# Differential attention in a decoder step: one mask, maximum and scaling for both components, rotation's additions on GpSimd, scores that wait per tile, weights transposed inside the value projection

## The reference, cut to what matters

```python
def diff_mix(q, k_parts, v_parts, masks, lam):          # per block of 128 queries
    scores = []
    for kp, mk in zip(k_parts, masks):
        s = jnp.einsum('bqhcd,bkhcd->bhcqk', q, kp).astype(F32) * ATTN_SCALE   # c: two components of 64
        s = jnp.where(mk, s, -jnp.inf)                  # causal
        scores.append(s)
    p = jax.nn.softmax(jnp.concatenate(scores, axis=-1), axis=-1)
    w = p[:, :, 0] - lam * p[:, :, 1]
    ...                                                 # o = w @ v

def diff_layer(...):
    q = rope(p[..., :QK_B].reshape(bsz, t_, H_B, 2, DK_B), pos)
    z = p[..., QK_B:]
    o = head_rmsnorm(attend(q, lam), subln) * (1.0 - lam_init)
    y = (o.reshape(bsz, t_, D_B).astype(x.dtype) * jax.nn.silu(z)) @ w_out
    return x + y
```

## Time and profile before

| | us |
|---|---|
| time, median of 3 runs | 2083.9 (2082.17 to 2084.59) |
| the profiled execution | 2088.54 |
| its span, first to last instruction | 2086.9 |
| TensorE busy in the span | 1802.2 (86%) |
| VectorE busy | 1164.0 (56%) |
| ScalarE busy | 821.2 (39%) |
| GpSimd busy | 402.1 (19%) |
| attention phase, from its first matmul to the last of its value projections | 955 to 1638 |

### The profile page before, as it was taken

How to read it: one execution, slowest core, us unless ns; L and a number is a source line. 1 busy time by engine, 2 the same in 40 slices (tenths; PEclk the granted TensorE clock), 3 DMA queues, 4 the chain that set the end, 5 groups by cost and what they waited for, 6 DMA issues and landing times. The chain is left out here.

```text
span 2086.9 us, 39907 instructions
## 1 busy us (share of the span) xinstructions
PE 1802.2 (86%) x12755; PEld 1650.1 (79%) x12755; DVE 1164.0 (56%) x3291; ACT 821.2 (39%) x2244; POOL 402.1 (19%) x847
## 2 busy tenths in 40 slices
PE   4399999999999585998999998999999688888598
PEld 4399899899999564997889898898989566665398
DVE  4444544444443354336767677676777466666533
ACT  5233333333333222133535435354354356666401
POOL 1022222222222121011313222122232100101101
PEclk8699999999999766998999999999999788989699
DMA  4213113113211134222111120211200267776522
GB/s 118 64 32 65 29 35 64 34 30 64 36 29 14 38 87 122 86 103 69 41 53 32 31 63 11 53 32 31 62 11 13 70 220 274 248 250 239 158 73 84
DMA packets 157013, 165.21 MB, mean 79 GB/s; under 512 B 12315, under 2 KB 134267, under 8 KB 156915
## 3 DMA queue, kind: packets, MB, share of 16 engines
q1 hardware_dynamic: 152610, 159.85, 25.9%
q0 software_dynamic: 1184, 4.23, 0.8%
q10 hardware_dynamic: 3120, 0.01, 0.1%
HBM read 138.69 MB, written 25.37 MB: 79 GB/s over the span
## 5 line engine op out<-in xcount | busy, mean ns | idle before, releaser
L837 PE MATMUL PS<-WH,XH 128*128 128x384 f32 (+1 forms) x1024 | 329.0, 321 | 2.7 <-DVE WORK L749 2.7
L837 PE MATMUL PS<-WL,XH 128*128 128x384 f32 (+1 forms) x1024 | 317.5, 310 | 0.0
L837 PE MATMUL PS<-WH,XL 128*128 128x384 f32 (+1 forms) x1024 | 317.2, 310 | 0.0
L837 PEld LDWEIGHTS PS<-WH,XH 128*128 128x128 f32 x1024 | 194.1, 190 | 3.6 <-DVE WORK L749 3.2
L1464 PE MATMUL PS<-WH,XH 128*128 128x256 f32 (+1 forms) x576 | 165.7, 288 | 36.0 <-DVE WL L1334 31.3
L837 PEld LDWEIGHTS PS<-WL,XH 128*128 128x128 f32 x1024 | 194.3, 190 | 0.0
L837 PEld LDWEIGHTS PS<-WH,XL 128*128 128x128 f32 x1024 | 193.7, 189 | 0.0
L1464 PE MATMUL PS<-WL,XH 128*128 128x256 f32 (+1 forms) x576 | 164.8, 286 | 0.0
L1464 PE MATMUL PS<-WH,XL 128*128 128x256 f32 (+1 forms) x576 | 163.6, 284 | 0.0
L1890 PE MATMUL PS<-WH,XH 128*128 128x256 f32 x512 | 154.9, 303 | 4.3 <-ACT WORK L1618 2.3
L1890 PE MATMUL PD<-WH,XH 128*128 128x256 f32 x512 | 151.0, 295 | 3.3 <-PEq L142 3.3
(11 more groups left out here) (368 smaller groups left out, 4645.6 us busy)
## 6 DMA issues: line engine op xcount, KB each, us to landing
RAW<-in_cache_k SPq DMA_DIRECT2D x64, 512.0 KB, 4.6
WORK<-in_cache_v SPq DMA_DIRECT2D x64, 512.0 KB, 4.4
RAW<-in_w_in_a SPq DMA_DIRECT2D x40, 512.0 KB, 6.2
RAW<-in_w_in_b SPq DMA_DIRECT2D x16, 512.0 KB, 6.5
RAW<-in_w_kv SPq DMA_DIRECT2D x16, 512.0 KB, 5.3
out<-WORK SPq DMA_DIRECT2D x16, 512.0 KB, 3.2
WORK<-in_x_prompt SPq DMA_DIRECT2D x8, 512.0 KB, 4.6
WORK<-d_G SPq DMA_DIRECT2D x8, 512.0 KB, 13.3
```

Source lines behind the costliest of these rows:

```text
L837: last = nc.tensor.matmul(bank[:, 0:n], x[:, k, tt], reg(w)[:, k, :], start=(i == 0), stop=(i == 3 * KT - 1))
```

## The change

It touches `attention_phase` alone, and one PSUM allocation that joins PD's two halves so that one instruction can address both components.

1. VectorE: mask, maximum and scaling of a tile are one instruction each for both components (`maxima`), so three instead of six. `weights` and `output`, which stood between the components, follow. The two reciprocals become one.
2. ScalarE: the exponential of c = 1 goes first, then the copy of the transposed weights, then c = 0; both wait for the joint scaling.
3. TensorE: `scores(t)` waits once for both exponentials of t-1, and for the rests of the tiles that it reads; the matmuls of the components alternate. The general wait before `scores(0)` goes, a smaller one stands in t = 1.
4. TensorE: `turn_weights(t-1)` moves from before the value projection of t+1 into its middle.
5. Rotation: the negative sine product is formed on VectorE, and two additions per tile move to GpSimd, which writes q and k to their places; the copy on GpSimd goes. VectorE's wait for its own rotation goes, and it waits for GpSimd before the next tile's products. SyncE waits for GpSimd before it sends keys.
6. The sample tile of sweep 1 is projected into bank B_O instead of PD, and some order in `sweep1` of VectorE and GpSimd changes.

```diff
-            QKR = take(2, 2, P)
+            QKR = take(2, P)
-            S = [PD[c][:, :, :].rearrange("p a n -> p (a n)") for c in range(2)]
+            S = PDT[:, :, :, :].rearrange("p c a n -> p c (a n)")
...
+                    def exponentials(h, t, c):
+                        n = (t + 1) * P
+                        act.activation(PR[:, c, 0:n], S[:, c, 0:n], ACT.Exp, scale=ATTN_SCALE, bias=nm[:, c:c + 1],
+                                       accum_out=sm[:, c:c + 1]).then_inc(ex, 1)
                     def sweep2(h, last):
...
-                            if 1 <= t < NT:
-                                weights(h, t - 1)
                             if t < NT:
+                                act.wait_ge(mxs, NT * h + t + 1)
+                                act.wait_ge(ww, NT * h + t)
+                                exponentials(h, t, 1)
+                                if t >= 1:
+                                    weights(h, t - 1)
                                 if t > 4:
                                     act.wait_ge(wt[1], 4 * h + (t - 4))
-                                for c in range(2):
-                                    act.wait_ge(mxs, 2 * (NT * h + t) + c + 1)
-                                    ...
+                                exponentials(h, t, 0)
...
-                        for t in range(NT):
-                            pool.wait_ge(rope, NB * h + t + 1)
-                            g.tensor_copy(KR[:, t, :], QKR[:, t % 2, 1, :]).then_inc(kr, 1)
-                            if t == 0 and before is not None:
+                        for t in range(NB):
+                            pool.wait_ge(rot, NB * h + t + 1)
...
+                            g.tensor_tensor(q_to..., RA[0:n, 0:4, :], RB[0:n, 0:4, :], ALU.add)
+                            g.tensor_tensor(k_to..., RA[0:n, 4:8, :], RB[0:n, 4:8, :], ALU.add).then_inc(rope, 1)
+                            if t == 1 and before is not None:
                                 root(before, NT - 1)
...
-                        links.link(v.tensor_tensor(RB[0:n, 1:8:2, :], src[:, 0:8:2, :], sin, ALU.mult))
-                        ...
-                        v.tensor_tensor(dst[:, 0:8:2, :], RA[0:n, 0:8:2, :], RB[0:n, 0:8:2, :], ALU.subtract)
-                        v.tensor_tensor(dst[:, 1:8:2, :], RA[0:n, 1:8:2, :], RB[0:n, 1:8:2, :], ALU.add)\
-                         .then_inc(rope, 1)
-                        dve.wait_ge(rope, NB * h + t + 1)
+                        dve.wait_ge(rope, NB * h + t)
+                        v.tensor_tensor(RA[0:n, :, :], src, cos, ALU.mult)
+                        v.scalar_tensor_tensor(RB[0:n, 0:8:2, :], src[:, 1:8:2, :], -1.0, sin, ALU.mult, ALU.mult)
+                        v.tensor_tensor(RB[0:n, 1:8:2, :], src[:, 0:8:2, :], sin, ALU.mult).then_inc(rot, 1)
...
+                    def maxima(h, t):
+                        n = (t + 1) * P
+                        dve.wait_ge(sc, NT * h + t + 1)
+                        links.link(v.tensor_tensor(S[:, :, n - P:n], S[:, :, n - P:n],
+                                                   cst[:, C_MB:C_MB + P].unsqueeze(1).to_broadcast([P, 2, P]), ALU.add))
+                        links.link(v.tensor_reduce(mx, S[:, :, 0:n], AX, ALU.max, negate=True))
+                        v.tensor_scalar(nm, mx, ATTN_SCALE, None, ALU.mult).then_inc(mxs, 1)
+                    def combine(h, t):
+                        n, b = (t + 1) * P, t % 2
+                        dve.wait_ge(ex, 2 * (NT * h + t) + 2)
+                        links.link(v.reciprocal(rc[:, b, :], sm))
+                        links.link(v.scalar_tensor_tensor(cf, sm[:, 0:1], nl, rc[:, b, 1:2], ALU.mult, ALU.mult))
+                        v.scalar_tensor_tensor(PR[:, 0, 0:n], PR[:, 1, 0:n], cf, PR[:, 0, 0:n], ALU.mult, ALU.add)...
                     def sweep2(h, last):
                         for t in range(NB):
                             if t < NT:
+                                maxima(h, t)
+                            if 4 < t < NT:
+                                weights(h, t - 1)
+                            if t >= 2:
                                 output(h, t - 2)
...
-                    heads(dve, sweep1, sweep2, tail, links, 10 + 8 * 2 * 2 + 16)
+                    heads(dve, sweep1, sweep2, tail, links, 1 + 8 * 4)
...
                     def scores(h, t):
+                        pe.wait_ge(ex, 2 * NT * h + 2 * t)
+                        for b in range(2):
+                            pe.wait_ge(trf[b], 4 * h + t // 2 + 1)
+                        for at in range(0, width, 512):
...
+                            for q, k in ((QTH, KTH), (QTH, KTL), (QTL, KTH)):
+                                for c in range(2):
...
                         for t in range(1, NT):
                             scores(h, t)
+                            values_free(t + 1)
+                            project(1, t + 1, B_V, (0, KT // 2))
...
                             turn_weights(h, t - 1)
-                            project_values(t + 1)
+                            project(1, t + 1, B_V, (KT // 2, KT))
                             if t >= 2:
                                 turn_output(h, t - 2)
                             weigh(h, t - 1)
```

166 lines of the change are left out of this document (75 added, 91 removed).

## The result

| | before | changed |
|---|---|---|
| median (lowest to highest), 4 runs each | 2083.03 us (2081.76 to 2084.59) | 2062.06 us (2061.76 to 2067.26) |
| ratio, 95% interval | | 0.9905 (0.9887 to 0.9922) |
| second comparison, on the chip of *rotation_dve*, *sep_cut_order* and *turn_first* | 2079.11 us | 2061.81 us, 0.9914 (0.9892 to 0.9936) |
| the profiled execution (its span) | 2088.54 us (2086.9) | 2067.26 us (2065.6) |
| attention phase, first projection to last output transposed | 696.0 us (955.21 to 1651.17) | 675.9 us (951.26 to 1627.12) |

The kernel became faster, inside the stated range (2036 to 2080) and inside the first case's own range, but by 21 us and not by the 32 of the sum. The attention phase alone gave 20.1 of it; the phases ahead of it were 4.0 shorter in that one execution and those behind it 2.8 longer, which the change doesn't touch.

The account below looks back on a forecast made before the run. It took VectorE's program fetch at the loop's return, a VectorE-ScalarE ring in sweep 2 and TensorE in sweep 1 as bounds. Terms summed to -32.4 us: 2088.5 to 2056.1, scaled to the runs' median 2052; range 2036 to 2080.

Parts of the forecast that it names:

- the first case: VectorE's late restart at the loop's return is gone; likeliest 2052 us, own range 2036 to 2068, chance 0.72.
- stall: Sweep 2 of heads 1 to 6: VectorE's program fetch at the loop's return disappears with a shorter loop; -38.4 us.
- ring: Sweep 2, VectorE and ScalarE: both exponentials now wait for the joint maximum; +1.4 us a head, +10 in all.
- last head's ring: Last head, without cuts: the general wait before its first scores goes and the end comes earlier; -1 us.
- end of sweep 2: TensorE's next-head projection follows the last exponential sooner, about 1.0 us in each of 7 heads; -7 us.
- the clock: TensorE's longer wait before `turn_output(5)` at sweep 2's end lowers its clock in one head of three; +4 us.
- 153 is nearer to the lower end: VectorE's loop of 153 counted instructions lies nearer 131 (no gap) than 203 (gap), so the gain is taken whole.
- that rival (2078): VectorE's fetch gap at the loop's return stays despite the shorter loop; 2078 us (2070 to 2086), chance 0.19.
- The rotation: Sweep 1: TensorE's next projection hides GpSimd's two additions per tile; 0 us, bounds 0 and +6.
- a longer sweep 1: Stated sign of error: the prediction is wrong if sweep 1 becomes longer; no size given.
- The transposes: `turn_weights` in the middle of TensorE's projection finds its weights ready; counted among the rest, 0 us.
- The rival on the other side: VectorE's fetch gap stays and TensorE's clock falls at the end of each sweep 2; 2101 us, chance 0.09.

Follow-up runs that it names:

- rotation_dve: Changed kernel with the rotation's two additions back on VectorE instead of GpSimd; 2087.0 us, ratio to before 1.0027.
- sep_cut_order: Changed kernel with a maximum per component, ScalarE's roundings ahead of the exponentials, and VectorE's output ahead of its copy of weights; 2028.43 us, ratio to before 0.9755.
- turn_first: Changed kernel with the transposes of the weights ahead of the value projection again, not in its middle; 2061.26 us, ratio to before 0.9907.
- before_joint: Kernel before with only VectorE's mask, maximum and scaling made one instruction each for both components; one execution, 2084.01 us.
- sep_max: Changed kernel keeping the joint mask, with a maximum and a scaling per component again, c = 1 first; 2034.51 us, ratio to before 0.9785.
- copy_early: Changed kernel with ScalarE's copy of the transposed weights ahead of both exponentials in tiles 4 to 7; 2042.64 us, ratio to before 0.9825.
- cut_early: Changed kernel with ScalarE's two roundings of the next head's weights ahead of the tile's exponentials; 2051.01 us, ratio to before 0.9874.
- pad12: Changed kernel with 12 tiny VectorE instructions added behind each tile's rests in sweep 1; one execution, 2083.13 us.
- all_three: Changed kernel with early roundings, the early copy of transposed weights in tiles 4 to 7, and a maximum per component; 2031.62 us, ratio to before 0.977.
- copy_sep: Changed kernel with a maximum per component and the early copy of transposed weights in tiles 4 to 7, roundings unmoved; 2040.04 us, ratio to before 0.9807.

## Why the prediction was right, and where it wasn't

The attention phase by the prediction's terms, from the two traces (first scores, exponentials and projections of each head), adds up as follows:

| step | forecast | measured |
|---|---|---|
| stall, heads 1 to 6 against head 0, with the tiles slowed behind it | -38.4 | -36.9 |
| ring, heads 0 to 6 | +10 | +12.1 |
| last head's ring | -1 | +1.1 |
| end of sweep 2 and sweep 1: last exponential to next scores, 7 times | -7 and 0 | 238.8 to 241.7, +2.9 |
| of that, the clock (two slow starts of 1.1) | +4 | +2.2 |
| first scores to first exponentials' end, eight times 2.72 to 2.60 | not in the sum | -0.9 |
| ahead of the first scores, behind the last exponential | not in the sum | +0.5, +1.1 |
| sum | -32.4 | -20.1, as by the phase's bounds |

*The stall* was right in place, cause and size: the entry is gone, head 2's gap is 2.27 for scores, and the clock of sweep 2 is 1.00. But the step that said it would go ("153 is nearer to the lower end") rested on a count that doesn't decide: 178 counted instructions stall and 200 don't. The outcome came out as forecast; that argument for it fell, so as far as it goes the outcome was luck. Both the additions' move and the joint maximum shortened the loop. The joint maximum without the move leaves the stall (before_joint, rotation_dve), and the move with separate maxima has none (sep_max). Where the loop lies and how many instructions of all kinds it has, the prediction had not looked at. The rule of the Trainium skill (*Runtime: NRT & Kernel Launch*, *Instruction fetch mechanics*) that a taken branch out of the current window forces a fetch agrees with these traces: with 5 packets in a turn there is a gap, without packets there is none. As the prediction applied it, the shorter loop would have left its window. That didn't follow without the loop's place and full length, and that rival (2078) fell.

*The ring* came out tile by tile: 5.11, 5.83, 6.57, 7.16, 7.77, 8.39 measured for t = 2 to 7, against 5.11, 5.82, 6.55, 7.17, 7.78, 8.40 from before's tiles with the forecast differences (5.56 + 0.26 and so on). Tile 1 was missed, 4.73 against 4.39, 0.34 a head, which makes the 2.1 us; before_joint has 4.38 there, so it isn't the joint maximum, and what it is stays open. The value taken for the joint maximum (the fixed part is saved once) was the right end of its bounds. But the term's name hid its larger part. By itself the joint maximum cost 0.6 a head (before_joint); the sum's 0.50 for the copy of the transposed weights, which the change put between the exponentials, is what copy_early gave back (0.4 to 0.5 in each of tiles 4 to 7). And the forecast didn't say how much the ring offers: the same 7.17 contained 0.5 of copy and 0.8 of maximum that could leave it.

*End of sweep 2, -7, is the step that failed.* It took two neighbours in time, the last matmuls of weights times values and the next projection, for the only cause and effect, because in the earlier trace rows the one runs into the other. The projection also waits for VectorE's last weight split, 0.11 ahead of it in both kernels, queued behind ScalarE's rounding, which is queued behind the exponentials. The change did move the matmuls of weights times values: in head 2 they begin 0.99 ahead of the exponential's end instead of 0.50. So half of the predicted 1.0 was there; ahead of them TensorE waits 1.61 us for VectorE's `o_transposed` and then 0.43 for ScalarE's copy of the transposed weights. Nothing in the change moved the split, so the gain was zero. With the roundings early the start did move, to 0.56, in the one head whose clock held.

*The rotation* was not free: 0.6 us a head against *rotation_dve*, 4 in all, inside the bound of +6, and TensorE does wait for the additions there, for a reason that the sum's cover had left out: the last tile has the sample's short projection behind it, not one of 2.95. Against the kernel before sweep 1 is only 0.14 longer where the clock holds, so other parts of the change gave some 0.5 a head that the sum had put at nothing. By the prediction's own sign, a longer sweep 1, it was wrong here, by that little. *The last head's* gain of 1 wasn't there either, because its ring has the joint maximum too; +1.1 is within the range given in the ring's paragraph. *The clock* was of the forecast's size, in one or two heads of seven; the wait before line 1936's successor was 1.6 us and not 2.1 (before, its 1.19 was for `o_transposed`, line 1787, not for `output(5)`), and the falls came at the end of sweep 2, while the windows read above stay at 1.00. *The transposes* were rightly put at nothing.

The rival on the other side (stall stays and clock falls, 2101) had no chance once the stall went; its clock half did appear, in cut_early. All in all the time lies inside the range because the stall, the largest term, was right; the 12 us between the sum and the phase are the missing 7, 2 of the ring, 2 of the last head and smaller terms of both signs. The low end of the range didn't matter, but it doesn't follow from its terms: without the falls (4) and with a ring better by 1 us a head (8), 2052 becomes 2040 and not 2036, and a joint maximum that loses its fixed part would add time.

## What to carry to other kernels

When an engine restarts late behind a hardware loop's return and no semaphore explains it, look at the instruction queue's packets in that turn, and try the loop with padding and without before you trust any count of instructions. Where two engines form a ring, list every instruction on it and ask of each if it can stand in the other engine's waiting time; that, and undoing the joint maximum, was worth more here (33 us) than the whole change. And when two instructions meet in a timeline, read all of the waits of the later one, on every engine, before you name its releaser: the profile put no name to it here ("issue"), and the end of a split 0.11 us earlier was the only trace of it.

## What the runs showed of the hardware that was not expected

The fetch at the loop's return doesn't follow the loop's length alone: 303 instructions paid it, 314 that began 21 instructions later in the program didn't. A turn that pays moves 5 packets, 0.04 MB; the restart took up to 5.2 us (pad12) to 6.3 us (before), and in all 24 cases came 1.9 to 2.1 us after the first packet's start. And TensorE's granted clock fell at the end of a sweep 2 in 17 places over all fourteen traces, only in kernels where TensorE waited twice there, 1.2 to 1.7 us and then 0.44 for ScalarE's copy (17 of their 49 places). No fall came in the kernels with one such wait (1.6 to 1.7 us in copy_early, sep_max, all_three and copy_sep, 1.2 to 1.4 in before and before_joint) or with waits of 1.1 and 0.3 (sep_cut_order). That is a coincidence of waits and falls, not a cause shown: cut_early has six falls in seven places and the changed kernel one or two, and why is open.
